# State-space mixing in one chunk of 256 tokens: decays from split products and ScalarE, outputs one tile later

## The reference

```python
SSD_CHUNK = 128
def ssd_chunked(x, dt, a, bm, cm):
    ...
    xd = (x * dt[..., None]).reshape(b, c, l, g, r, p)
    da = (dt * a).reshape(b, c, l, g, r).transpose(0, 1, 3, 4, 2)
    a_cs = jnp.cumsum(da, axis=-1)
    decay_in = jnp.exp(jnp.where(causal, a_cs[..., :, None] - a_cs[..., None, :], -jnp.inf))
    cb = jnp.einsum('bclgn,bcsgn->bcgls', cm, bm)
    y_diag = jnp.einsum('bcgrls,bcsgrp->bclgrp', cb[:, :, :, None] * decay_in, xd)
    ...
    return (y_diag + y_off).reshape(b, s, h, p)

    y = ssd_chunked(xs, dt, a, bm, cm) + d_skip.astype(jnp.float32)[:, None] * xs
    y = y.reshape(b, s, SSD_D_INNER) * jax.nn.silu(z.astype(jnp.float32))
    y = rms_norm(...)          # over each group's 512 channels
    return y.astype(h.dtype) @ w_out
```

## Time and profile before

| | |
|---|---|
| median of 3 runs | 1568.57 us (1568.09 to 1569.09) |
| the profiled execution | 1568.66 us, its span 1566.9 us |
| PE busy | 1545.3 us, 99% of the span |
| DVE busy | 1303.5 us, 83% |
| ACT busy | 1100.2 us, 70% |
| POOL busy | 67.9 us, 4% |
| the four tiles with the core, and Z3 | 447.2 to 545.6 us of the span |

### The profile page before, as it was taken

The page is one execution under the profiler, slowest core; times in us unless marked ns, Lnnn a source line. Parts: engine busy times, 40 slices in busy tenths (PEclk is TensorE's granted clock), DMA queues, the critical chain, the costliest instruction groups (busy, mean ns, idle before and its releaser), DMA issues.

```text
span 1566.9 us, 24788 instructions
## 1 busy us (share of the span) xinstructions
PE 1545.3 (99%) x9121; PEld 1348.4 (86%) x9121; DVE 1303.5 (83%) x1589; ACT 1100.2 (70%) x1295; POOL 67.9 (4%) x57
## 2 busy tenths in 40 slices
PE   9999999999999999999999999999999999999997
PEld 7879999999999998888888888888888888888886
DVE  6766655555799877999999999999999999999996
ACT  5676444444566656788888878888888888788785
POOL 0001100100001000000000000000000000000000
PEclk9999999999999999999999999999999999999999
DMA  9335445445343359999999999999999999999980
GB/s 345 111 135 185 171 164 207 168 168 175 142 162 108 109 211 396 378 390 379 393 385 358 394 385 353 393 388 353 393 388 350 394 390 350 394 388 352 394 325 12
DMA packets 188260, 455.72 MB, mean 291 GB/s; under 512 B 4089, under 2 KB 4587, under 8 KB 188187
## 3 DMA queue, kind: packets, MB, share of 16 engines
q1 hardware_dynamic: 185082, 444.48, 76.9%
q0 software_dynamic: 2928, 10.17, 2.5%
q10 hardware_dynamic: 176, 0.07, 0.0%
HBM read 449.45 MB, written 5.26 MB: 290 GB/s over the span
## 4 chain that ended last, share of the span: by engine, by line
issue 56%; PE 36%; DVE 4%; POOL 2%; ACT 1%; DMA 1%; POOLq 0%; ACTq 0%; DVEq 0%
PE bank L683 36%; DVE split_mem L1622 1%; POOL mem L657 1%; POOL out L649 1%; DMA h_rows<-mem 1%; DVE mem L1809 1%; DVE mem L1777 0%; DVE mem L1821 0%; ACT split_mem L1173 0%; DMA rows<-norm_mix 0%; DVE mem L1648 0%; DVE split_mem L2184 0%; DVE mem L1579 0%; DVE split_mem L1600 0%; DVE mem L1589 0%
## 5 line engine op out<-in xcount | busy, mean ns | idle before, releaser
L683 PE MATMUL bank<-split_mem 128*128 128x256 f32 (+1 forms) x8064 | 1442.4, 339 | 3.9 <-DVE split_mem L2184 1.3
L683 PEld LDWEIGHTS bank<-split_mem 128*128 128x128 f32 x8064 | 1243.7, 190 | 171.1 <-issue 6.5
L2184 DVE TENSOR_TENSOR split_mem<-mem,split_mem 128x1024 fp32r<-128x1024 f32 x668 | 806.6, 1223 | 66.0 <-ACT split_mem L1507 24.6
L1507 ACT CAST split_mem<-mem 128x1024 fp32r<-128x1024 f32 x672 | 707.1, 1054 | 188.2 <-PE bank L683 187.2
L1622 DVE TENSOR_TENSOR split_mem<-mem,split_mem 128x1024 fp32r<-128x1024 f32 x172 | 213.3, 1254 | 118.7 <-ACT split_mem L1173 118.6
L1173 ACT CAST split_mem<-mem 128x1024 fp32r<-128x1024 f32 x172 | 177.6, 1044 | 133.2 <-PE bank L683 129.8
L683 PE MATMUL bank<-mem 128*64 128x128 f32 (+6 forms) x382 | 45.3, 309 | 3.7 <-DVE mem L1556 1.5
L683 PEld LDWEIGHTS bank<-mem 128*64 128x64 f32 (+2 forms) x382 | 33.7, 165 | 10.5 <-issue 7.1
L1514 ACT ACTIVATE mem<-bank,small 96x512 f32<-96x512 f32 x56 | 38.4, 685 | 2.1 <-DVE small L2129 2.1
L2191 DVE TENSOR_TENSOR mem<-mem,bank 96x512 f32<-96x512 f32 x56 | 37.9, 676 | 0.0
L1777 DVE SCALAR_TENSOR_TENSOR mem<-mem,colA 128x253 f32<-128x253 f32 (+2 forms) x72 | 31.5, 479 | 4.0 <-ACT mem L1257 3.1
(11 more groups left out here) (203 smaller groups left out, 509.2 us busy)
## 6 DMA issues: line engine op xcount, KB each, us to landing
mem<-moe_w_gate SPq DMA_DIRECT2D x56, 2048.0 KB, 9.3
mem<-moe_w_up SPq DMA_DIRECT2D x56, 2048.0 KB, 9.9
mem<-moe_w_down SPq DMA_DIRECT2D x56, 2048.0 KB, 9.9
mem<-ssd_w_in SPq DMA_DIRECT2D x10, 2048.0 KB, 7.9
mem<-ffn_w_gate SPq DMA_DIRECT2D x7, 2048.0 KB, 8.3
mem<-ffn_w_up SPq DMA_DIRECT2D x7, 2048.0 KB, 7.9
mem<-ffn_w_down SPq DMA_DIRECT2D x7, 2048.0 KB, 7.9
mem<-attn_w_in SPq DMA_DIRECT2D x5, 2048.0 KB, 11.2
```

Of the source, the lines that this page charges most:

```text
L683: return nc.tensor.matmul(o, lhsT, rhs, start=start, stop=stop, skip_group_check=shared)
L1507: nc.scalar.copy(wsplit[:, EXPERT_BUFFER[n % SPLITS], 0, :].rearrange("p (k n) -> p k n", n=w.shape[2]), quarter(w, q)).then_inc(w_hi, 1)
L2184: tt_(lo, quarter(w, q), hi.bitcast(F32), ALU.subtract).then_inc(w_lo, 1)
```

## The change

The mixer takes the 256 tokens as one chunk. The chunk state, the exponentials of the running sums, the copy of B and all of POOL's work for the core are gone. The running sums come in two forms: by token (`acs`, as before) and by head, one row each (`acsT`, 64 rows: the high parts of 32 heads and their remainders); `pick` is a matrix of ones and zeros, and one fp32r product of a broadcast column of it by `acsT` spreads a head's 256 running sums over all partitions (`spread`). ACT takes them out of PSUM with Relu(bias - x), bias being the head's own running sum per token (16 instructions for a group), and then makes two exponentials of 4x384 columns with scale -1. DVE multiplies those by the masked cb in two instructions. PE makes 16 products for the outputs instead of 24 (`group_output`), and they stand in the next tile, behind its quarter 0.

The diff, cut to what is spoken of:

```diff
@@ banks
         B.plan("dt", 1), B.plan("acs", 2)
+        CORE_BANKS = [(0, 3), (4, 5), (0, 3), (4, 5)]
         for g in range(GROUPS):
-            B.plan(("xn", g, 0), 7), B.plan(("cb", g), 6), B.plan(("xn", g, 1), 4 if g else 1)
+            B.plan(("xn", g, 0), 7), B.plan(("cb", g), 6), B.plan(("xn", g, 1), 1)
...
-            B.plan(("state", g), 1)
+                for half in range(2):
+                    B.plan(("y", g - 1, half), 1 + half)
             for half in range(2):
-                for c in range(TT):
-                    B.plan(("ab", g, half, c), 4 + 2 * half + c)
-            for half in range(2):
-                B.plan(("y", g, half), 1 + half)
+                for i in range(2):
+                    B.plan(("ab", g, half, i), 7 - i)
@@ POOL
-            for g in range(GROUPS):
-                ... (xw: one product of 128x512; C by the exponentials: two of 128x512)
@@ PE
+            def spread(g, half):
+                B.released(pe, "acs")
+                for i in range(2):
+                    B.claim(pe, ("ab", g, half, i))
+                    for j in range(2):
+                        h = g * HPG + 4 * half + 2 * i + j
+                        last = mm(bank[7 - i][:, j * T:(j + 1) * T], pick[:, h:h + 1].broadcast_to([2 * SH, P]),
+                                  acsT, True, True)
+                    B.finish(last, ("ab", g, half, i))
+
+            def group_output(g):
+                for half in range(2):
+                    B.claim(pe, ("y", g, half))
+                    pe.wait_ge(m_ready, 2 * g + half + 1)
+                    for q in range(4):
+                        o = bank[1 + half][HD * (q % 2):HD * (q % 2 + 1), (q // 2) * T:(q // 2 + 1) * T]
+                        h = 4 * half + q
+                        mm(o, xd[:, g % 2, h * HD:(h + 1) * HD], mix[:, h, 0:T], True, False)
+                        last = mm(o[:, P:T], xd[:, g % 2, 512 + h * HD:512 + (h + 1) * HD], mix[:, h, T:T + P],
+                                  False, True)
+                    B.finish(last, ("y", g, half))
...
-                for q in range(2):
-                    project(tile, (0, 3), q)
-                ... (state; 16 products into the four banks "ab")
-                for q in range(2, 4):
-                    project(tile, (0, 3), q)
-                ... (24 products of y)
+                for q in range(4):
+                    project(tile, CORE_BANKS[g], q)
+                    if q == 0 and g:
+                        group_output(g - 1)
+                    if q < 2:
+                        spread(g, q)
@@ ACT
-            def core(g):
-                ... (copy of the state, four exponentials of 512, two of 512 out of PSUM)
+            def core(g, half):
+                B.released(act, "acs")
+                if g:
+                    B.ready(act, ("y", g - 1, 1))
+                for i in range(2):
+                    B.ready(act, ("ab", g, half, i))
+                    for j in range(2):
+                        h = 4 * half + 2 * i + j
+                        src = bank[7 - i][:, j * T:(j + 1) * T]
+                        fn(mix[:, h, 0:T], src, ACT.Relu, bias=acs[:, 0, g * HPG + h:g * HPG + h + 1], scale=-1.0)
+                        last = fn(mix[:, h, T:T + P], src[:, P:T], ACT.Relu,
+                                  bias=acs[:, 1, g * HPG + h:g * HPG + h + 1], scale=-1.0)
+                    B.release(last, ("ab", g, half, i))
+                ...
+                fn(o, o, ACT.Exp, scale=-1.0).then_inc(dec_ready, 1)
@@ DVE
-            def core(g):
-                ... (16 subtractions out of PSUM, 4 products of 512)
+            def core(g, half):
+                dve.wait_ge(dec_ready, 2 * g + half + 1)
+                o = mix[:, 4 * half:4 * half + 4, :]
+                tt_(o, o, cbm[:, g % 2, :].unsqueeze(1).broadcast_to([P, 4, T + P]), ALU.mult).then_inc(m_ready, 1)
```

219 lines of the change are left out of this document (82 added, 137 removed).

## The result

The changed kernel took 1572.38 us (median of 8 runs, 1571.01 to 1574.50), the kernel before 1568.53 us (8 runs, 1568.09 to 1569.60): a ratio of 1.0025 with a 95% interval of 1.0015 to 1.0035. The change costs 3.85 us. The forecast was 1573.2 us, 4.5 us more than before.

The account below looks back on a forecast made before the run. PE and DVE were taken to share the bound in X3, Z0 and Z1. Laid out link by link, the five tiles X3 to Z3 summed to +4.5 us on the profiled 1568.66: 1573.2 us, range 1565.5 to 1580.

Parts of the forecast that it names:

- (a): PE's second spread needs banks 7 and 6, released by the Relus of the first half; 4.7 us wait in X3.
- (d): Outputs y use bank 1, so PE waits for DVE's core_inputs of that tile; 4.8 us in Z1.
- 14 us of gain: By PE alone the four tiles would save 3.4 us each, some 14 us.
- the running sums: Longer product on PE, once, before X3: 0.65 us, costed at nothing because DVE and ACT run 3 us behind PE.
- A Relus' pair: ACT's Relus out of PSUM: 0.40 us for 256 columns, 0.27 for 128, a head 0.67, four heads 2.7 us.
- The product: DVE's product of 1536 columns: 1.75 us undisturbed by POOL, 2.6 us at three times the old median.
- the exponential: ACT's exponential of 1536 columns: 1.48 us, two per tile.
- The outputs: PE's output products of 3072 columns: 3.1 us, bounds 2.6 and 5.1 us.
- PE's pace: Rival: the loop is hidden and PE sets the tiles' time, with X3's wait staying: 1559 us, chance 0.17.
- the draw: Rival: the loop binds but shorter, each half's Relus 2.2 us, giving back 4 us: 1569 us, chance 0.18.
- The falling clock: Rival: PE's clock falls to half speed behind its waits in X3 and Z1: +2.6 us, 1575.8 us, chance 0.15.

Follow-up runs that it names:

- longer sums: Changed kernel with the two products for the running sums by head made four times instead of once: 1573.59 us, ratio 1.0031.
- early Relus: Changed kernel with the first half's Relus ahead of the table load in X3, Z0, Z1, and in X3 ahead of conv_silu(8): 1572.15 us, ratio 1.0011.
- shared reading: Changed kernel with DVE taking the two heads of bank 6 by subtraction and min, ACT keeping those of bank 7: 1571.71 us, ratio 1.0014.
- the banks alone: Changed kernel with outputs y in the two banks of the previous tile's projection: 1572.87 us, ratio 1.0022.
- moved taps: Changed kernel with DVE's conv_taps(10) and conv_taps(11) ahead of the two products with the masked cb of Z0: 1567.87 us, ratio 0.9995.
- run 3: This name does not occur in the text given, which numbers no run 3, so no change or measured time can be stated for it.

## Why the prediction was right, step by step

The forecast was laid out link by link, so it can be checked link by link. Times from X3's start in us, forecast, measured, and measured in the trace with the longer sums, whose code is the same here:

| | forecast | changed kernel | longer sums |
|---|---|---|---|
| spread of X3's second half done | 13.6 | 13.6 | 13.3 |
| y begins in Z0 | 26.1 | 25.8 | 25.3 |
| y begins in Z1 | 50.8 | 51.2 | 49.6 |
| y begins in Z2 | 71.9 | 71.7 | 70.3 |
| the mean of the first group begins | 86.4 | 85.4 | 84.0 |
| Z3 ends | 102.8 | 101.7 | 100.3 |

The mechanism is borne out: waits (a) and (d), their releasers, and a loss of some microseconds where PE's work alone promised 14 us of gain. The closeness of the number is in part luck. The forecast sum has full clock throughout and nothing for the running sums. With the quarters of Z0 at full clock the same code takes 2.0 us more than before from X3 to Z3's end, not 4.5; the running sums added 0.8 us that the sum didn't have, and in the trace of the changed kernel the slow clock in Z0 added another 1.4 us. Two of the signs named ahead failed: X3 was to take near 19 us and took 21.3, and Z1 was to be the longest and Z0 was (22.9 for 21.7 us). X3's excess of 1.9 us over the forecast tile is that of its last two quarters at the slow clock (7.84 us for 5.99).

- **Condition (a)** is there: PE waits 3.08 + 0.39 us in X3, where 4.7 was forecast in one piece. The first part of the spread can begin when bank 7 alone is free, two heads earlier; the second bank still waits, so that the spread ends when forecast. The early Relus and the shared reading show that their start sets this wait and not their length.
- **Condition (d)** is there in Z1 and Z2 with L1793 as the releaser, as forecast, but not in Z0, where 2.3 us of it were forecast (471.1 to 473.4) and PE, behind X3's slow quarters, came too late to wait. The 4.8 us of Z1 are 2.40, and 4.17 in the trace whose quarters of Z0 were fast: PE came to it late from Z0, at the slow clock. To gain more than 0.5 us from its removal (a) has to go too. The prediction priced each wait by itself and had nothing on how (a) and (d) cover one another, which is why 1 to 2 us were expected of the banks alone.
- **The prices.** A Relus' pair starts 0.37 and 0.25 us apart (460.34, 460.71, 460.96), a head 0.62 us, for 0.40 + 0.27. Two groups by form, 447 to 540 us (busy, mean ns of one, idle before):

```profile
L1806 DVE TENSOR_TENSOR mem<-mem 128x1536 f32<-128x1536 f32 x8 | 14.1, 1759 | 19.8 <-ACT mem L1291 19.8
...
L1291 ACT ACTIVATE mem<-mem 128x1536 f32<-128x1536 f32 x8 | 11.9, 1488 | 0.7
```

The product was put at 1.75 us and took 1.76 in all eight; the exponential at 1.48 and 1.49. The products of before scattered from 0.68 to 1.78 us for 512 columns beside POOL; with POOL's work gone, eight of eight agree within 2 ns. That agrees with the Trainium skill ("GPSIMD Engine Reference", Specifications), which has GpSimd in the way of DVE instructions with two SBUF inputs, though no run here puts the new product beside POOL. DVE's idle time ahead of the product, 19.8 us in eight waits for the exponential, is the loop seen from DVE. The outputs took 2.87 us for 3.1. Their upper bound in the prediction, 5.1 us, should have read 5.2 (3.49 us for 2048 columns, times 1.5); nothing hangs on it.
- **The mis-sized terms.** The four tiles and Z3 cost 3.39 us for 4.5. Most of the difference, 0.8 us, lies between y in Z2 and the mean (13.7 us for 14.5): 0.3 us are the output, whose successor starts 2.80 us behind it, and 0.4 us the stretch of exponential, cast, Relus and exponential on ACT, 6.42 us (527.90 to 534.32) for 6.8, since an instruction there starts before the one ahead of it is recorded as ended (the cast 1.40 us behind the start of an exponential of 1.49). The running sums were costed at nothing with 0.65 us at most; they cost 0.79 us in the trace, and repeating them showed it all on the path. The reason given ("DVE and ACT run 3 us behind PE there") was read at X3, 35 us later, and is no reason at the sums: from them to X3 PE works without a wait (34.82 us in one row, from 415.45), so its own length sets the time, and DVE waits at the sums themselves (2.05 us in the changed kernel). These errors have opposite signs, and the time came out 0.8 us from the forecast.
- **The rivals.** PE's pace is out (1559 us, a launch without waits in Z0 to Z2): the waits are there. So is the draw (1569 us) by the interval, whose low end is 1.0015, or 1570.9 us. The falling clock came true as a fact: the wait of X3 is followed by a clock of one half, the lower of the two levels, 1.2 GHz. Windows of the changed kernel behind it:

```profile
461.84:463.70 1.86, 1.47 (x4) 0.97 (x4) 0.00 (x0) 1.77 (x5) 0.00 (x0) 0.50 1.04 389
463.72:467.00 3.28, 3.28 (x16) 3.28 (x16) 2.45 (x2) 3.28 (x8) 0.00 (x0) 0.50 0.91 343
467.00:471.40 4.40, 4.40 (x36) 4.40 (x34) 2.20 (x2) 3.38 (x6) 0.00 (x0) 0.90 0.00 0
```

Its price of 2.6 us did not: DVE's chain hid the 1.9 us that X3's quarters lost (y in Z0 begins without a wait and 0.3 us ahead of the forecast), and what was lost in Z0 showed as 1.05 us of DVE waiting for PE ahead of scale_z in Z1, a wait that the trace with the fast quarters of Z0 doesn't have. The Trainium skill ("TensorE: Matmul & The Clock Gate", Why this matters for your kernels) warns of such gaps; the trace agrees that the clock was lower behind them, but not behind every one, as the quarters of Z0 at 8.62 and 6.01 us behind nearly the same waits show. The traces put the price at 1.4 to 1.6 us in a launch with slow quarters in Z0; what it is in the median isn't shown.

## What to carry to other kernels

Where several engines share a bound, lay the order of all of them on the times of the old trace, link by link; that forecast the waits and the sign of the change, and the time to 0.8 us with some luck, whereas the work saved on PE said 14 us of gain. When the work is moved to another engine, ask where in that engine's stream it lands: here the whole cost came back by order alone, when twelve of DVE's taps went into its waits, and some of it when the Relus went ahead of the silu and the table load. A removed wait that gains nothing may still be half of a pair; take away the one that took its place before judging it. And before a difference between two traces is credited to an edit, look at a second trace of the same code: here the stretch in question differs by 1.4 us between two.

## What the runs showed of the hardware

- Behind PE's wait of 3.08 us the granted clock was 0.50 from 461.84 to 467.00 us (windows above); in the kernel before, with no more than 1.1 us free in a tile, it was 1.00 throughout. A wait doesn't decide it alone: behind 2.40 us of it the outputs in Z1 took 4.55 us in the changed kernel, and 2.87 behind the same wait in the one with shared reading. The same code in Z0 ran at the full clock in one trace and not in another (6.01 and 8.62 us for two quarters, above). What decides it isn't shown.

```profile
499.48 2.87 PE L672 MATMUL bank<-mem 128*64 128x256 f32 x32 [2.39 <-DVE mem L1794]
```

- The start of a launch differs from run to run. Windows of 17 to 25 us of three traces, code that is the same in each: the kernel before, the changed kernel, and that with moved taps.

```profile
17.00:25.00 8.00, 8.00 (x66) 7.93 (x66) 5.03 (x7) 3.25 (x9) 0.70 (x1) 1.00 1.05 387
```

```profile
17.00:25.00 8.00, 8.00 (x51) 7.24 (x50) 5.59 (x8) 2.50 (x7) 0.70 (x1) 0.79 1.05 388
```

```profile
17.00:25.00 8.00, 8.00 (x39) 7.10 (x38) 5.49 (x8) 2.44 (x7) 0.70 (x1) 0.57 1.05 389
```

Of the changed kernel and its twelve variants, with that of the longer sums left aside, the traces at 1.00 (seven) begin X3 at 448.0 to 448.5 us, those at 0.79 (four) at 449.9 to 450.2, the one at 0.57 at 451.5. What decides it wasn't tried. On average it is worth 1.8 us at 0.79 and 3.3 us at 0.57, as much as the change: a single pair of profiles must be cleared of it before it is read, by a point ahead of the changed code.
- Relu runs under the silu table and under that of the exponentials alike: moved ahead of the load, it caused none of its own (1341 instructions on ACT in both).
